# Stick-breaking attention with its mask added by a matmul, its suffix sums in two rounded passes, and the outputs of two heads side by side

## What is computed

```python
z = einsum('bhqd,bhkd->bhqk', q[:, :, t0:t1], k[:, :, :t1]) * dh ** -0.5
causal = arange(t1)[None, :] < arange(t0, t1)[:, None]
log_1m = where(causal, log_sigmoid(-z), 0.0)
log_after = cumsum(log_1m, axis=3, reverse=True) - log_1m
w = where(causal, exp(log_sigmoid(z) + log_after), 0.0)
out = einsum('bhqk,bhkd->bhqd', w, v[:, :, :t1])
```

## Time and profile before

| | |
|---|---|
| timed runs | 3440.98, 3442.36, 3443.94 us; median 3442.36 |
| profiled execution, first to last instruction | 3437.4 us |
| TensorE busy | 3220.2 us (94%) |
| VectorE busy | 1686.9 us (49%) |
| GpSimd busy | 1315.3 us (38%) |
| ScalarE busy | 1194.9 us (35%) |
| mean granted clock of TensorE | 0.972 of full speed |
| DMA | 352.99 MB, mean 103 GB/s |

### The profile page before, as it was taken

The page is one execution under the profiler, slowest core; times in us unless marked ns, Lnnn a source line. Parts: engine busy times, 40 slices in busy tenths (PEclk is TensorE's granted clock), DMA queues, the critical chain, the costliest instruction groups (busy, mean ns, idle before and its releaser), DMA issues. The chain is left out here.

```text
span 3437.4 us, 43582 instructions
## 1 busy us (share of the span) xinstructions
PE 3220.2 (94%) x16752; PEld 2534.5 (74%) x16752; DVE 1686.9 (49%) x2853; ACT 1194.9 (35%) x1541; POOL 1315.3 (38%) x719
## 2 busy tenths in 40 slices
PE   7998999989988899998988998999999997989998
PEld 6864788877768688886873377888899783378887
DVE  5534342426685573744937526634355737431111
ACT  3254322224744322223234433222344324442222
POOL 3314444444451434342315542343401414544443
PEclk9999999999999899999999999999999998999999
DMA  7510344432101243441100022444454210022321
GB/s 273 207 42 37 114 169 144 188 120 84 64 13 40 94 172 129 173 151 61 62 26 1 1 86 104 162 155 170 144 176 165 86 38 1 25 86 83 108 86 67
DMA packets 54648, 352.99 MB, mean 103 GB/s; under 512 B 5856, under 2 KB 6880, under 8 KB 19552
## 3 DMA queue, kind: packets, MB, share of 16 engines
q1 hardware_dynamic: 54208, 348.79, 27.6%
q10 hardware_dynamic: 288, 2.10, 0.2%
HBM read 348.77 MB, written 2.10 MB: 102 GB/s over the span
## 5 line engine op out<-in xcount | busy, mean ns | idle before, releaser
L393 POOL TENSOR_TENSOR W_LO<-ring,W_HI 128x2048 fp32r<-128x2048 f32 (+1 forms) x177 | 729.2, 4120 | 1049.2 <-ACT W_HI L381 1049.2
L449 PE MATMUL PS<-H_HI,W_HI 128*128 128x512 f32 (+1 forms) x1888 | 712.1, 377 | 30.9 <-DVE H_LO L872 24.3
L451 PE MATMUL PS<-H_HI,W_LO 128*128 128x512 f32 (+1 forms) x1888 | 702.7, 372 | 0.0
L450 PE MATMUL PS<-H_LO,W_HI 128*128 128x512 f32 (+1 forms) x1888 | 702.3, 372 | 0.0
L381 ACT ACTIVATE W_HI<-ring 128x2048 fp32r<-128x2048 f32 (+1 forms) x214 | 366.2, 1711 | 458.7 <-PE PS L439 417.8
L449 PEld LDWEIGHTS PS<-H_HI,W_HI 128*128 128x128 f32 x1888 | 359.2, 190 | 94.8 <-issue 33.5
L451 PEld LDWEIGHTS PS<-H_HI,W_LO 128*128 128x128 f32 x1888 | 358.7, 190 | 62.9
L450 PEld LDWEIGHTS PS<-H_LO,W_HI 128*128 128x128 f32 x1888 | 359.3, 190 | 59.2 <-issue 0.2
L914 DVE SCALAR_TENSOR_TENSOR PS<-ring,SC,PS 128x256 f32<-128x256 f32 x774 | 379.2, 490 | 27.2
L437 PE MATMUL PS<-HID_HI,W_HI 128*128 128x512 f32 (+1 forms) x880 | 325.3, 370 | 4.9 <-DVE W_LO L393 4.0
L439 PE MATMUL PS<-HID_HI,W_LO 128*128 128x512 f32 (+1 forms) x880 | 323.7, 368 | 0.0
(11 more groups left out here) (407 smaller groups left out, 5395.1 us busy)
## 6 DMA issues: line engine op xcount, KB each, us to landing
ring<-w_tiles SPq DMA_DIRECT2D x271, 1024.0 KB, 4.8
ring<-d_tiles SPq DMA_DIRECT2D x80, 704.0 KB, 4.1
X<-xT SPq DMA_DIRECT2D x1, 2048.0 KB, 16.2
WORK<-rope_tables ACTq DMA_DIRECT2D x2, 1024.0 KB, 4.8
outT<-H SPq DMA_DIRECT2D x8, 256.0 KB, 2.2
X<-ctxT SPq DMA_DIRECT2D x1, 1024.0 KB, 8.8
CN<-consts SPq DMA_DIRECT2D x1, 931.0 KB, 7.5
PR<-params SPq DMA_DIRECT2D x1, 465.5 KB, 3.3
```

The source lines that it names most:

```text
L393: eng.tensor_tensor(W_LO[:, b, 0:w], ring[:, g % SLOTS, 0:w], W_HI[:, b, 0:w].bitcast(F32), ALU.subtract).then_inc(sig("tile_split"), 1)
L449: pe.matmul(to, hi[:, cols(k, j)], x_hi(k), start=k == 0, stop=False)
L450: pe.matmul(to, hi[:, cols(k, j)], x_lo(k), start=False, stop=False)
L451: mm = pe.matmul(to, lo[:, cols(k, j)], x_hi(k), start=False, stop=k == n - 1)
```

## The change

- A constant `future` is added: 0 where the query is later than the key, -1e30 elsewhere. `z(h)` adds it to the four diagonal blocks with four fp32r matmuls (identity times `future`). GpSimd's selects and the function `pool_stick` go.
- Softplus is split as the large matmuls' operands are: ScalarE rounds it to `STICK_HI` (`rounded`), VectorE writes the rest over it (`rest`, to `STICK_LO`, which lies where softplus lay). `sums(h)` makes each of its ten products twice in fp32r, once with each part. `ident`, `future`, `negtri` and `negones` are converted to fp32r by ScalarE at the start of the phase.
- `outputs(n)` makes two heads at once, alternating between them block by block, at every second head; the copy out of PSUM takes both heads and moves to VectorE.
- ScalarE's order becomes rounded(h), softplus(h + 1), weights(h); VectorE's rest(h), rotate(h), softplus(h + 1), and after even heads the copy.

```diff
+                STICK_LO = sticks.enter_context(nc.sbuf_tensor("STICK_LO", [P, 2, 1280], F32R))
+                sticks.enter_context(nc.sbuf_tensor("STICK_GAP", [P, 2 * 1280], F32R))
+                STICK_HI = sticks.enter_context(nc.sbuf_tensor("STICK_HI", [P, 2, 1280], F32R))
+                STICK_CONSTS = sticks.enter_context(nc.sbuf_tensor("STICK_CONSTS", [P, 4, P], F32R))
...
 
+        NEGTRI_R, NEGONES_R, IDENT_R, FUTURE_R = [STICK_CONSTS[:, n, :] for n in range(4)]
+
         def pe_stick(pe):
             def z(h):
                 if h >= 2:
@@ -1716,31 +1723,39 @@
                 r = slice((h % 2) * 64, (h % 2) * 64 + 64)
                 for i in (0, 1, 3, 2):
                     a, w = sb_bank(h, i), T - i * P
-
-                    mm = pe.matmul(PS[:, a:a + w], QK1[r, 12 + h // 2, i * P:(i + 1) * P],
-                                   QK1[r, 8 + h // 2, i * P:T], start=i != 3, stop=True, skip_group_check=True)
+                    pe.matmul(PS[:, a:a + w], QK1[r, 12 + h // 2, i * P:(i + 1) * P],
+                              QK1[r, 8 + h // 2, i * P:T], start=i != 3, stop=False, skip_group_check=True)
+                if h == 0:
+                    pe.wait_ge(sig("stick_consts"), 2)
+                for i in range(NT):
+                    a = sb_bank(h, i)
+                    mm = pe.matmul(PS[:, a:a + P], IDENT_R, FUTURE_R, start=False, stop=True, skip_group_check=True)
                 mm.then_inc(sig("z_ready"), 1)
 
             def sums(h):
-                pe.wait_ge(sig("softplus_masked"), h + 1)
+                pe.wait_ge(sig("sticks_split"), h + 1)
+                if h == 0:
+                    pe.wait_ge(sig("stick_consts"), 4)
                 for i in (0, 1, 3, 2):
                     for j in range(i, NT):
                         a = sb_bank(h, i) + (j - i) * P
                         w = T - j * P
-                        mm = pe.matmul(PS[:, a:a + w], const("negtri") if j == i else const("negones"),
-                                       SP_[h % 2][:, OFFS[j]:OFFS[j] + w], start=False, stop=True, skip_group_check=True)
+                        for part in (STICK_HI, STICK_LO):
+                            mm = pe.matmul(PS[:, a:a + w], NEGTRI_R if j == i else NEGONES_R,
+                                           part[:, h % 2, OFFS[j]:OFFS[j] + w], start=False, stop=True, skip_group_check=True)
                 mm.then_inc(sig("sticks_ready"), 1)
 
-            def outputs(h):
-                pe.wait_ge(sig("sticks_masked"), h + 1)
-                if h >= 2:
-                    pe.wait_ge(sig("stick_heads_copied"), h - 1)
-                off = (h % 2) * 64
+            def outputs(n):
+
+                pe.wait_ge(sig("sticks_read"), 2 * n + 2)
+                if n:
+                    pe.wait_ge(sig("stick_heads_copied"), n)
                 for i in range(NT):
-                    o = 3072
-                    mm = pe.matmul(PS[off:off + 64, o + i * P:o + T], V1[:, i, 512 + h * 64:512 + (h + 1) * 64],
-                                   SW[h % 2][:, OFFS[i]:OFFS[i] + T - i * P], start=i == 0, stop=i == NT - 1,
-                                   skip_group_check=True)
+                    for h in (2 * n, 2 * n + 1):
+                        off = (h % 2) * 64
+                        mm = pe.matmul(PS[off:off + 64, 3072 + i * P:3072 + T], V1[:, i, 512 + h * 64:512 + (h + 1) * 64],
+                                       SW[h % 2][:, OFFS[i]:OFFS[i] + T - i * P], start=i == 0, stop=i == NT - 1,
+                                       skip_group_check=True)
                 mm.then_inc(sig("stick_heads_ready"), 1)
 
             def swap(n):
@@ -1756,9 +1771,9 @@
                     z(h + 1)
                 swap(h)
                 sums(h)
-                if h >= 1:
-                    outputs(h - 1)
-            outputs(7)
+                if h % 2 == 0 and h:
+                    outputs(h // 2 - 1)
+            outputs(3)
 
         def act_stick(act, chain):
             def softplus(h):
@@ -1770,27 +1785,25 @@
                 chain(act.activation(L, L, ACT.Exp, scale=-1.0))
                 act.activation(L, L, ACT.Ln, bias=SM[:, 1:2]).then_inc(sig("log_ready"), 1)
 
+            def rounded(h):
+                act.wait_ge(sig("softplus_ready"), h + 1)
+                act.activation(STICK_HI[:, h % 2, :], SP_[h % 2], ACT.Copy).then_inc(sig("sticks_rounded"), 1)
+
             def weights(h):
                 act.wait_ge(sig("sticks_ready"), h + 1)
                 if h >= 2:
-                    act.wait_ge(sig("stick_heads_ready"), h - 1)
+                    act.wait_ge(sig("stick_heads_ready"), h // 2)
                 a = (h % 2) * 1536
                 act.activation(SW[h % 2], PS[:, a:a + SBW], ACT.Exp).then_inc(sig("sticks_read"), 1)
 
-            def copy(h):
-                off = (h % 2) * 64
-                act.wait_ge(sig("stick_heads_ready"), h + 1)
-                act.activation(H[off:off + 64, 4 + h // 2, 0:T], PS[off:off + 64, 3072:3072 + T],
-                               ACT.Copy).then_inc(sig("stick_heads_copied"), 1)
-
+            for n, name in enumerate(("ident", "future", "negtri", "negones")):
+                act.activation((IDENT_R, FUTURE_R, NEGTRI_R, NEGONES_R)[n], const(name), ACT.Copy).then_inc(sig("stick_consts"), 1)
             softplus(0)
             for h in range(8):
+                rounded(h)
                 if h + 1 < 8:
                     softplus(h + 1)
                 weights(h)
-                if h >= 1:
-                    copy(h - 1)
-            copy(7)
 
         def dve_stick(dve, chain):
             def rotate(n):
@@ -1801,31 +1814,32 @@
                 chain(dve.tensor_tensor(c, c, cos, ALU.mult))
                 dve.tensor_tensor(c, c, tmp, ALU.add)
 
-            for h in range(8):
+            def softplus(h):
                 dve.wait_ge(sig("log_ready"), h + 1)
                 a = (h % 2) * 1536
-
                 dve.scalar_tensor_tensor(out=SP_[h % 2], in0=PS[:, a:a + SBW], scalar=0.0, in1=SP_[h % 2],
                                          op0=ALU.max, op1=ALU.add).then_inc(sig("softplus_ready"), 1)
+
+            def rest(h):
+                dve.wait_ge(sig("softplus_ready"), h + 1)
+                dve.wait_ge(sig("sticks_rounded"), h + 1)
+                dve.tensor_tensor(STICK_LO[:, h % 2, :], SP_[h % 2], STICK_HI[:, h % 2, :].bitcast(F32),
+                                  ALU.subtract).then_inc(sig("sticks_split"), 1)
+
+            def copied(n):
+                dve.wait_ge(sig("stick_heads_ready"), n + 1)
+                dve.tensor_copy(H[:, 4 + n, 0:T], PS[:, 3072:3072 + T]).then_inc(sig("stick_heads_copied"), 1)
+
+            softplus(0)
+            for h in range(8):
+                rest(h)
                 rotate(h)
-
-        def pool_stick(pool):
-            def keep_past(buf):
-
-                for i in range(NT):
-                    v = buf[:, OFFS[i]:OFFS[i] + P]
-                    ins = pool.affine_select(out=v, in_=v, compare_op=ALU.is_gt, fill=0.0, base=0,
-                                             pattern=[[1, P]], channel_multiplier=-1)
-                return ins
-            def soft(h):
-                pool.wait_ge(sig("softplus_ready"), h + 1)
-                keep_past(SP_[h % 2]).then_inc(sig("softplus_masked"), 1)
-            soft(0)
-            for h in range(8):
                 if h + 1 < 8:
-                    soft(h + 1)
-                pool.wait_ge(sig("sticks_read"), h + 1)
-                keep_past(SW[h % 2]).then_inc(sig("sticks_masked"), 1)
+                    softplus(h + 1)
+                if h % 2 == 0 and h:
+                    copied(h // 2 - 1)
+            copied(3)
+
...
+    put("future", np.where(j > i, 0, NEG))
```

More of the change, by code:

```diff
@@ L42 @@
 _at = 0
-for _name, _w in [("ident", P), ("ones", P), ("tri", P), ("negtri", P), ("negones", P), ("perm_a1", P),
+for _name, _w in [("ident", P), ("ones", P), ("tri", P), ("negtri", P), ("negones", P), ("future", P), ("perm_a1", P),
                   ("perm_64", P), ("perm_32", P), ("causal", P), ("bands", 3 * P),
@@ L132, in build_program @@
             BIG = part("BIG", [P, 32 * T])
+            with ExitStack() as sticks:
+                STICK_LO = sticks.enter_context(nc.sbuf_tensor("STICK_LO", [P, 2, 1280], F32R))
+                sticks.enter_context(nc.sbuf_tensor("STICK_GAP", [P, 2 * 1280], F32R))
+                STICK_HI = sticks.enter_context(nc.sbuf_tensor("STICK_HI", [P, 2, 1280], F32R))
+                STICK_CONSTS = sticks.enter_context(nc.sbuf_tensor("STICK_CONSTS", [P, 4, P], F32R))
             WORK = part("WORK", [P, 9216])
@@ L3199, in _ @@
                     ph.end(pool)
-                    pool_stick(pool)
                     ph.end(pool)
```

## The result

The changed kernel takes 3448.98 us (median of 14 runs, 3445.96 to 3466.44) against 3442.36 for the kernel before (14 runs beside them, 3440.46 to 3444.96). The ratio is 1.0024, 95% interval 1.0015 to 1.0032: slower by a quarter of a percent. The forecast was 3444.4, with a range of 3434.5 to 3455. Two runs of the kernel before beside the last experiments took 3507.80 and 4630.24 us, at mean clocks of 0.905 and 0.65; every comparison leaves them out.

A forecast was written before the change was run, and what follows sets the result against it. TensorE at full clock was taken to bound the stage's middle. Stage: 80.8 + 1.4 + 10.2 + 0.2 = 92.6 us against 90.6, 2 us more, so 3444.4 us from a median of 3442.4; range 3434.5 to 3455.

The forecast's parts named there:

- The ring at full clock: Scores wait for ScalarE's weights of two heads earlier: heads of 8.13 and 10.28 us alternate, 18.4 a pair against 20.1.
- The sum of 80.8 us for the stage at full clock: Whole stage: 60.44 us through the rings, 10.23 for the last even head's work, 10.1 for the tail; 90.6 before.
- The sums: TensorE, each head: 20 rounded matmuls take 2.80 us with the switch from the swap, instead of 4.43; 1.63 less.
- The rival of dear short matmuls: Sums and mask: 128-column matmuls cost four times the assumed 0.11 us, some 21 us more, 3466 us; chance 6%.
- The mask: TensorE behind each head's scores: four more matmuls, 0.45 us; constant conversions on ScalarE, 0.3 each, are covered.
- The outputs: TensorE, per pair of heads: alternating products run side by side, 2.32 us instead of 4.88, 1.15 a head less.
- the rival in series: Outputs of a pair do not overlap: four times 2.3 us more, 3453.6 us in all; chance 5%.
- The clock: Idle gaps on TensorE lower the granted clock: 1.4 us at the start, six drops of 1.7 us, 10.2.
- the forecast case: Clock in the stage: five drops of 1.2 us to seven of 2.1, time 3439 to 3449 us; chance 50%.
- the rival of longer stretches: Clock stays down longer: each of seven gaps costs 3.4 us, stage 106.2, time 3458 us; chance 22%.
- the first of its rivals: Clock stays up because gaps of 1.5 us are too short: stage 82.4, time 3434.2 us; chance 17%.
- The rest: Loading 64 KB more constants costs 0.2 us; GpSimd's selects were off the path and leave no trace in the sum.

The follow-up runs named there:

- the version that holds the clock: Changed kernel with four weight buffers, unused matmuls filling gaps and twelve more ahead of the first sums: 3434.82 us, ratio 0.9979 to the kernel before.
- the second profile: Changed kernel run once more, unedited: 3451.8 us, ratio 1.0027 to the kernel before; in this profile the stage took 111.4 us.
- four buffers alone: Changed kernel with four buffers for ScalarE's weights instead of two, without filling: 3447.73 us, ratio 1.0009 to the kernel before.
- The same filling: Changed kernel with five unused 512-column matmuls in each of seven TensorE gaps: 3440.72 us using 128 array rows, 3446.1 using 64.

## Why the prediction was right, point by point

- **The ring at full clock.** Right to 0.1 us: 10.36 and 8.17 measured, 10.28 and 8.13 forecast. The sum of 80.8 us for the stage at full clock was seen only with other edits, in the version that holds the clock: 15.88 us to the third scores (15.49 forecast), 44.98 for the five rings behind them (44.95), and 18.91 for the end (20.33, with two buffers where this version has four), 79.8 in all. Drawn down from the two profiles of the changed kernel, at 0.38 us for each of the 30 us at half clock, 94.3 becomes 82.8. The 9.8 us that were to be saved if the clock stays up set this against a stage of before with its own low stretches; by the prediction's own rows these cost 1.67 + 1.70 us, so at full clock on both sides the change is worth some 6.4.
- **The sums.** Two rounded passes took with the swap 3.74 us against 3.76 forecast and 5.39 before. The missing row, matmuls of 128 columns, turned out cheap: where the clock is 1.00, the starts of matmuls of 128 columns in the sums are 0.06 and 0.11 us apart in turn. So the lower bound of 0.10, taken from matmuls of one column, was wrong, and the 0.11 a little high. The rival of dear short matmuls is out.
- **The mask.** 2.85 us for scores and mask against 2.80. The four conversions took 0.91 us together, 0.23 each against 0.3, and were covered. What the mask costs in time could not be seen: without it the mean was the same within the scatter.
- **The outputs.** Side by side, 2.37 us a pair against 2.32. In series it is 3.93 and not 4.6; the rival in series would have cost 1.6 a pair instead of 2.3.
- **The wait moved where it was said**, to the scores behind ScalarE's weights, with 1.33 to 1.52 us idle, and ScalarE behind the outputs in even heads.
- **The clock.** The right mechanism, and mis-sized. The term was 1.4 us for the start and 10.2 for six drops of 1.7. In the first profile the cost was 94.3 - 80.8 = 13.5, near the 11.6, but made up otherwise, so that the nearness is in part luck: the start and the stretch that carried over the third scores cost 6.9, where 1.4 and one drop of 1.7 were put, and only three later drops came, for 6.5, where five of 1.7 were put. In the second profile the cost was 30.6. The median of the timed runs is 6.6 us above before, and 8.8 when taken again, where 2 were forecast. It fell into the stated range, but not into the case called likeliest (within 0.2%, 52%): the ratio of 1.0024 (1.0015 to 1.0032) lies rather in the case slower by over 0.2%, which had 30%. The measured value lies between the forecast case and the rival of longer stretches, which had 22%. What I missed is that a drop can last twice as long (6.9 us, with no gap in it) and can carry over the next gap (17 us), and that the clock can be low from the first scores on.
- **The rule of the Trainium skill** (TensorE: Matmul & The Clock Gate, section "HAM oscillation — how this bites in real kernels"), by which gaps this short would not matter, does not describe this stage: five of six gaps of 1.46 to 1.48 us and three of those of 1.3 to 1.5 in the changed kernel were followed by 1.2 GHz, and filling five times 0.23 us into them took some 9 us off the time. The measurement decides. The prediction says that by this rule the time would be that of the second case; it is the first of its rivals, in which the clock stays up (3434.2 us), that is meant.
- **The rest.** 0.2 us for the wider constants can't be told from none (3443.75 against 3443.09). That GpSimd's selects were off the path holds for the middle only: by the earlier trace rows the first sums of before wait for them, and the trace has the four selects from 199.75 to 201.71, 1.96 us on the path. The sum did not use this, as it was built up anew.
- **What stays open.** Why four buffers alone gained 4 to 6 us, and not the 9 of theory, is explained only by the clock of 0.75 in their profile; what decides, run by run, whether a gap of 1.3 to 1.5 us is followed by a drop, and whether the clock falls at the first scores already, was not tried. Nor is it shown whether the rows that the scores use have a part in it.

## What to carry to other kernels

Taking work off an engine that is then found waiting may cost more than it gives where the granted clock falls behind the new gaps, as here: read the granted clock by stretch beside the busy times, in more than one profile, before trusting a gain. If the ring of waits leaves a gap, first put work of the kernel's own into it (the swap, a third and fourth buffer); even matmuls without use paid here. Work that is moved within a ring that another engine sets does not shorten the wait there. The products of two heads on different halves of the columns ran side by side, most of all when they alternated (2.37 us against 3.93).

## What the runs showed of the hardware that was not expected

- Leaving out 32 short matmuls saved nothing: the runs fell into two groups, 3443 to 3446 and 3456 to 3461 us, and the stage's granted clock in the profile, a run of the slower group, was 0.68.
- Gaps of 1.46 to 1.48 us on TensorE were followed by some 7 us at 1.2 GHz in five of six cases, gaps of 0.34 us or less in none.
- One program, two profiles on different occasions: 94.3 and 111.4 us for the same stage, at 0.84 and 0.66.
- The same filling took 3446.1 us on 64 rows and 3440.7 on 128, though in the profile the clock stayed at 1.00 over the gaps with either.
- Output products of two heads issued one head after the other still overlap by 0.8 us of 4.7.
